# First mixer's attention: the two heads of a pair scored side by side, and the causal mask added into the gate row

## The reference

```
c = jnp.cumsum(logf, axis=-1)
...
    logits = jnp.einsum('bhqd,bhkd->bhqk', qb, k) * scale + cb[..., None] - c[:, :, None, :]
    allowed = (kpos[None, :] <= qpos[:, None]) & (valid[None, :] | (kpos[None, :] == qpos[:, None]))
    p = jax.nn.softmax(jnp.where(allowed[None, None], logits, NEG), axis=-1)
    return jnp.einsum('bhqk,bhkd->bhqd', p, v)
```

## Time and profile before

| | us |
|---|---|
| median of 3 runs | 3825.36 (3823.08 to 3827.70) |
| the profiled execution | 3827.49 |
| its span in the trace | 3825.7 |
| PE busy | 3763.7 |
| DVE busy | 1361.9 |
| POOL busy | 1045.1 |
| ACT busy | 757.2 |

### The profile page before, as it was taken

The page is one execution under the profiler, slowest core; times in us unless marked ns, Lnnn a source line. Parts: engine busy times, 40 slices in busy tenths (PEclk is TensorE's granted clock), DMA queues, the critical chain, the costliest instruction groups (busy, mean ns, idle before and its releaser), DMA issues.

```text
span 3825.7 us, 42159 instructions
## 1 busy us (share of the span) xinstructions
PE 3763.7 (98%) x17657; PEld 2652.7 (69%) x17657; DVE 1361.9 (36%) x2155; ACT 757.2 (20%) x1343; POOL 1045.1 (27%) x919
## 2 busy tenths in 40 slices
PE   8999999999999999999999999999999999999999
PEld 7888677775554588874565444478887557748888
DVE  3221210311121322135634300168823274338861
ACT  2000251222300100012332310010012355230000
POOL 4554100000000155522442100046641020016663
PEclk9999999999999999999999999999999999999999
DMA  4222443223131233222323222223223410023322
GB/s 134 82 86 83 85 67 58 36 34 44 50 66 66 81 85 88 86 84 76 99 83 105 66 77 77 77 77 89 86 91 108 77 45 4 6 56 88 89 83 72
DMA packets 368031, 281.83 MB, mean 74 GB/s; under 512 B 11011, under 2 KB 359811, under 8 KB 367844
## 3 DMA queue, kind: packets, MB, share of 16 engines
q1 hardware_dynamic: 367556, 278.88, 27.5%
q10 hardware_dynamic: 288, 0.27, 0.0%
HBM read 276.44 MB, written 2.69 MB: 73 GB/s over the span
## 4 chain that ended last, share of the span: by engine, by line
PE 97%; DVE 1%; ACT 1%; issue 0%; DMA 0%; POOL 0%; SPq 0%; DVEq 0%; ACTq 0%
PE psum L604 41%; PE psum L1995 14%; PE psum L1309 6%; PE psum L2188 3%; PE psum L1430 3%; PE psum L2886 3%; PE psum L1344 2%; PE psum L1091 1%; PE psum L1121 1%; PE psum L3726 1%; PE psum L1982 1%; PE psum L1087 1%; PE psum L1162 1%; PE psum L3461 1%; PE psum L573 1%; PE psum L2972 1%
## 5 line engine op out<-in xcount | busy, mean ns | idle before, releaser
L604 PE MATMUL psum<-work 128*128 128x256 f32 (+1 forms) x2400 | 551.4, 381 | 0.0
L523 POOL TENSOR_TENSOR work<-weight_ring 128x512 f32<-128x512 f32 x132 | 163.2, 1236 | 1376.5 <-PE psum L604 735.0
L604 PEld LDWEIGHTS psum<-work 128*128 128x128 f32 x2400 | 456.0, 190 | 66.0
L604 PE MATMUL psum<-work,weight_ring 128*128 128x256 f32 (+1 forms) x2080 | 481.8, 381 | 0.0
L604 PE MATMUL psum<-normalized,weight_ring 128*128 128x256 f32 (+1 forms) x2016 | 468.2, 382 | 2.9 <-DVE normalized L724 2.9
L1995 PE MATMUL psum<-normalized,weight_ring 128*128 128x512 f32 x1024 | 451.1, 596 | 0.0
L604 PEld LDWEIGHTS psum<-work,weight_ring 128*128 128x128 f32 x2080 | 395.2, 190 | 57.2
L604 PEld LDWEIGHTS psum<-normalized,weight_ring 128*128 128x128 f32 x2016 | 383.6, 190 | 61.4 <-DVE normalized L724 4.5
L1995 PEld LDWEIGHTS psum<-normalized,weight_ring 128*128 128x128 f32 x1024 | 192.3, 191 | 228.8 <-issue 227.7
L748 DVE TENSOR_TENSOR work<-work,psum 128x512 f32<-128x512 f32 (+1 forms) x100 | 68.7, 687 | 641.7 <-PE psum L604 641.7
L682 ACT ACTIVATE work<-psum 128x256 f32<-128x256 f32 (+1 forms) x100 | 38.5, 385 | 1094.2 <-PE psum L604 1094.2
(11 more groups left out here) (518 smaller groups left out, 4915.9 us busy)
## 6 DMA issues: line engine op xcount, KB each, us to landing
weight_ring<-in_w_in SPq DMA_DIRECT2D x73, 1024.0 KB, 7.7
weight_ring<-in_w_ffn_in SPq DMA_DIRECT2D x88, 512.0 KB, 5.1
weight_ring<-in_ffn_w_up SPq DMA_DIRECT2D x44, 512.0 KB, 4.6
weight_ring<-in_ffn_up SPq DMA_DIRECT2D x44, 512.0 KB, 5.0
weight_ring<-in_w_ffn_out SPq DMA_DIRECT2D x16, 1024.0 KB, 5.2
weight_ring<-in_w_out SPq DMA_DIRECT2D x12, 1024.0 KB, 5.1
work<-decay_sums SPq DMA_DIRECT2D x16, 512.0 KB, 4.1
weight_ring<-in_w_proj_b SPq DMA_DIRECT2D x8, 1024.0 KB, 5.1
```

Source lines behind the costliest of these rows:

```text
L523: own(pool.tensor_tensor(s1, a21, a22, ALU.add))
L604: last = pe.matmul(K.ps[:, self.BANK[m] * T:self.BANK[m] * T + self.H], left(m, p), right(pe, m, p), start=first and p == 0, stop=last_par ...
```

## The change

Of the attention:

- `units()` lists a pair's units by query block from the last to the first, and the two heads of a block next to each other
- the scores of two units (one block, both heads) are issued together at every even turn (`scores_pe`), in pieces of at most 256 columns, head 0 and head 1 in turn, into banks 0 and 1; they wait until DVE has scaled both units before
- the causal mask's product on PE is gone; DVE adds the mask into the gate row's diagonal block ahead of each unit
- the gate rows, the meta scores and a pair's end stand at other turns: the even head's row at turn 7 of the pair before, the odd head's at turn 0 right behind the scores, the meta scores at turn 6 of the pair before, a pair's end one turn earlier each

Of the scan: DVE masks the scb products of both tiles of a pair first and does the rest of both after.

```diff
-        return [(p, h, i) for p in range(FOX_PAIRS) for h in range(2) for i in range(NT)]
+        return [(p, h, i) for p in range(FOX_PAIRS) for i in reversed(range(NT)) for h in range(2)]
...
-                if s > 1:
-                    pe.wait_ge(*S["scaled"](s - 1))
-                pe.matmul(K.bank(s % 2, (i + 1) * P), A(self.q + p * T + i * P, P, half(h)), A(self.k + p * TM, (i + 1) * P, half(h)),
-                          start=True, stop=False, skip_group_check=True)
-                pe.matmul(K.bank(s % 2, P, P, i * P), K.ident[:, :], K.causal[:, :], start=False, stop=True, skip_group_check=True)\
-                    .then_inc(S["scored"].h, 1)
+            more = p + 1 < FOX_PAIRS
+            if s < n and s % 2 == 0:
+                self.scores_pe(pe, s)
+            if s < n and rel == 0:
+                self.forget_bias_pe(pe, 2 * p + 1)
             self.side_until(side, (s + 4) * SIDE)
+            if more and rel == 6:
+                self.meta_scores_pe(pe, p + 1)
+            if more and rel == 7:
+                self.forget_bias_pe(pe, 2 * p + 2)
...
+        if s:
+            pe.wait_ge(*S["scaled"](s))
+        for c in range(0, width, HALF_BANK):
+            w = min(HALF_BANK, width - c)
+            for h in range(2):
+                last = pe.matmul(K.bank(h, w, P, c), A(self.q + p * T + i * P, P, half(h)), A(self.k + p * TM + c, w, half(h)),
+                                 start=True, stop=True)
+                if c + w == width:
+                    last.then_inc(S["scored"].h, 1)
...
+                if s:
+                    dve.wait_ge(*S["scaled"](s))
+                diagonal = A(self.ncb + h * T + i * P, P)
+                own(dve.tensor_tensor(diagonal, diagonal, K.causal[:, :], ALU.add))
+                own.wait()
                 dve.wait_ge(*S["scored"](s + 1))
                 if s > 2:
                     dve.wait_ge(*S["turned"](s - 2))
...
-        for t in N:
+        for both in (N[0:2], N[2:4]):
+            for t in both:
+                b = 4 * (t % 2)
+                dve.wait_ge(*Z["scb"](t + 1))
```

More of the change, by code:

```diff
@@ L876 @@
 PAIR_UNITS = 2 * NT
+HALF_BANK = 256
 SIDE = 7
@@ L1188, in attention_pe, with scores_pe @@
             if s >= PAIR_UNITS:
-                if rel == 2:
+                if rel == 1:
                     self.meta_turn_pe(pe, p - 1)
-                if rel == 4:
+                if rel == 3:
                     self.meta_values_pe(pe, p - 1)
-                if rel == 6:
+                if rel == 5:
                     self.turn_y_pe(pe, p - 1)
-            if rel == 5 and p + 1 < FOX_PAIRS:
-                self.forget_bias_pe(pe, 2 * p + 2)
+    def scores_pe(self, pe, s):
+        K, A, S = self.K, self.A, self.s
+        p, _, i = self.units()[s]
+        width = (i + 1) * P
+        if s:
[7 more added lines that the diff above has]
+                    last.then_inc(S["scored"].h, 1)
     def forget_bias_pe(self, pe, head):
@@ L1201, in forget_bias_pe @@
         p = head // 2
[L1202 to L1206, removed]
+        if head % 2:
+            pe.wait_ge(*S["ncb_copied"](head))
+        else:
             pe.wait_ge(*S["meta_biased"](p + 1))
[L1208 to L1211, removed]
         row = bass.AP(K.ident, head, [[P, FOX_HEADS], [0, P]])
@@ L1216, in meta_scores_pe @@
         K, A, S = self.K, self.A, self.s
[L1217 to L1221, removed]
+        if p == 1:
+            pe.wait_ge(*S["ncb_copied"](2))
+        elif p > 1:
             pe.wait_ge(*S["y_ready"](p - 1))
@@ L1243, in turn_y_pe @@
         pe.wait_ge(*S["tails"](p + 1))
[L1244 removed]
+        pe.wait_ge(*S["ncb_copied"](min(2 * p + 4, FOX_HEADS)))
         pe.wait_ge(*S["meta_copied"](p + 1))
@@ L1496, in attention_act @@
                 Ls = A(self.L + (s % 3) * T, (units[s][2] + 1) * P)
+                if rel == 0:
+                    self.forget_bias_act(act, 2 * p + 1)
                 act.wait_ge(*S["scaled"](s + 1))
@@ L1499, in attention_act @@
                     .then_inc(S["probs"].h, 1)
-                if rel == 1:
-                    self.forget_bias_act(act, 2 * p + 1)
+                if rel == 7 and p + 1 < FOX_PAIRS:
+                    self.forget_bias_act(act, 2 * p + 2)
             if s >= PAIR_UNITS:
-                if rel == 1:
+                if rel == 0:
                     mm = A(self.mm + ((p - 1) % 2) * P, P)
@@ L1506, in attention_act @@
                     act.activation(mm, mm, ACT.Exp, scale=-1.0).then_inc(S["meta_probs"].h, 1)
-                if rel == 2:
+                if rel == 1:
                     act.wait_ge(*S["meta_turned"](p))
                     act.activation(A(self.mt + ((p - 1) % 2) * P, P), K.bank(5, P), ACT.Copy).then_inc(S["meta_copied"].h, 1)
-                if rel == 6:
+                if rel == 5:
                     act.wait_ge(*S["y_turned"](p))
                     act.activation(A(self.q + (p - 1) * T, T), K.bank(5), ACT.Copy).then_inc(S["y_ready"].h, 1)
-            if rel == 5 and p + 1 < FOX_PAIRS:
-                self.forget_bias_act(act, 2 * p + 2)
             for end, name, at in ends:
@@ L1524, in forget_bias_act @@
         if head > 1:
-            act.wait_ge(*S["scaled"](head // 2 * PAIR_UNITS - (4 if head % 2 == 0 else 0)))
+            act.wait_ge(*S["scaled"](head // 2 * PAIR_UNITS - (1 if head % 2 == 0 else 0)))
         act.activation(A(self.ncb + (head % 2) * T, T), self.K.bank(5), ACT.Copy).then_inc(S["ncb_copied"].h, 1)
@@ L1662, in attention_dve @@
         dve.wait_ge(*S["line_stored"](16))
+        self.meta_scores_dve(dve, own, 0)
         for s in range(n + 8):
@@ L1667, in attention_dve @@
                 c, w = self.column(s), (i + 1) * P
-                if rel == 0:
-                    self.meta_scores_dve(dve, own, p)
-                if i == 0:
+                if i == NT - 1:
                     dve.wait_ge(*S["ncb_copied"](2 * p + h + 1))
+                if s:
[3 more added lines that the diff above has]
+                own.wait()
                 dve.wait_ge(*S["scored"](s + 1))
@@ L1677, in attention_dve @@
                                          accum_out=A(self.stat_min + c, 1)).then_inc(S["scaled"].h, 1)
+                if rel == 6 and p + 1 < FOX_PAIRS:
+                    self.meta_scores_dve(dve, own, p + 1)
+                if rel == 7:
+                    self.meta_less_dve(dve, p)
             if s >= PAIR_UNITS:
-                if rel == 0:
-                    self.meta_less_dve(dve, p - 1)
-                if rel == 3:
+                if rel == 2:
                     self.total_dve(dve, own, p - 1)
-                if rel == 5:
+                if rel == 4:
                     self.tail_dve(dve, p - 1)
@@ new lines, in scan_dve @@
+        for both in (N[0:2], N[2:4]):
+            for t in both:
+                b = 4 * (t % 2)
+                dve.wait_ge(*Z["scb"](t + 1))
+                dve.tensor_tensor(A.two(self.si + t * 2 * T, self.rr + t * 2 * T, BLOCKS, 2 * CHUNK, CHUNK),
+                                  K.ps[:, b * T:(b + 2) * T].rearrange("p (x b n) -> p x b n", b=2, n=CHUNK),
+                                  mask(0, 2).rearrange("p x (b n) -> p x b n", n=CHUNK), ALU.mult).then_inc(Z["scb_masked"].h, 1)
+            for t in both:
+                b = 4 * (t % 2)
+                ab = self.bank_pair(b + 2, b + 3)
+                dve.tensor_tensor(self.heads(self.st, t), ab, self.masks_of(4), ALU.mult)
+                dve.wait_ge(*Z["scc"](t + 1))
+                dve.wait_ge(*Z["be_ready"](t + 1))
+                dve.tensor_tensor(self.heads(self.r, t), ab, self.masks_of(5), ALU.mult)
+                dve.tensor_tensor(self.heads(self.k, t), ab, self.masks_of(6), ALU.mult).then_inc(Z["ab_masked"].h, 1)
+                products = K.ps[:, b * T:(b + 2) * T].rearrange("p (x b n) -> p b x n", b=2, n=CHUNK)
+                dve.tensor_tensor(by(A(self.ar + t * T, T), CHUNK), products[:, 0], mask(2), ALU.mult)
+                dve.tensor_tensor(A.blocks(self.rr + t * 2 * T + CHUNK, BLOCKS, 2 * CHUNK, CHUNK), products[:, 1], mask(3), ALU.mult)\
+                   .then_inc(Z["scc_masked"].h, 1)
```

9 lines of the change are left out of this document (2 added, 7 removed).

## The result

The changed kernel took **3781.39 us** (median of 4 runs, 3778.22 to 3782.29) against 3824.96 for before on the same chip. The ratio is 0.9884 with a 95% interval of 0.9867 to 0.9901, 43.6 us less. The forecast was 3780, from a gain of 45.3.

What follows compares the result with a forecast made beforehand. PE was taken to bound the kernel, with slack on DVE. Attention's 41.3 us (13.8 + 11.4 + 17.1, less losses) plus the scan's 4.0 made 45.3, from 3825.4 to 3780 us; range 3773 to 3794.

Steps and rivals of the forecast that it cites:

- rival A: Whole kernel: the forecast itself, all three parts of the change pay, 3774 to 3786 us; chance 0.70.
- The mask, 13.8 us: Attention on PE: dropping the mask's product removes 64 units of 0.215 us, 13.8 us saved.
- The row halves, 17.1 less 0.7: Attention scores on PE: two heads side by side cost one head's columns, 17.1 us saved, less 0.7 for lost overlap.
- Changes of height, 11.4: Attention on PE: changes of weight height fall from 145 to 88, at 0.20 us each, 11.4 us saved.
- 1.0 (0.7 + 0.2 + 0.1): Attention losses: 0.7 us of lost overlap, 0.2 net behind turn 56, 0.1 for the start.
- The split at turn 56: Attention's end, without side work: PE saves 5.4 us, waits add 2.8, a shorter drain returns 2.6; net loss 0.2.
- The hand-over: Scores' stricter wait for DVE: hidden by 3.0 us of side work; rival D, waits at all 32 groups, 3793 us, 0.09.
- The scan, 4.0: Scan: masking both tiles first ends the last masks 3.3 us earlier; up to 1.6 more from the clock; 4.0 taken.
- a sign that the prediction had ruled out: Scan: second scc should start about 0.5 us behind the first, and no record be stretched to 0.42.
- Strict order (B): Attention scores: matmuls start only in program order, costing 6.0 us in all, 3786 us; chance 0.10.
- no overlap (C): Attention scores: neighbouring pieces block each other, so only 13.8 + 11.4 + 4.0 = 29.2 us are saved, 3796; chance 0.06.

Runs made afterwards that it cites:

- experiment 4: Changed kernel with the causal mask's product back on PE and no mask addition on DVE: 3800.66 us, attention stage 314.6 (311.2 without the low clock).
- experiment 2: Changed kernel with head 1's scores reading head 0's partitions, so both use the same row half: 3801.03 us, attention stage 315.5 (312.1 at full clock).
- experiment 5: Changed kernel with DVE adding the mask four or eight times over instead of once: 3793.19 and 3801.57 us.
- experiment 1: Each edit alone against the kernel before (3827.73 us): changed attention with old scan order 3783.80; old attention with new scan order 3823.56.
- heads-apart run: Changed kernel with all of head 0's score pieces issued first, then all of head 1's, instead of in turn: 3779.47 us, attention stage 295.3.
- four additions: Changed kernel with DVE adding the mask four times over, about 1.0 us more on DVE ahead of each unit: 3793.19 us.

## Why the prediction was right

The time was 3781.4 for 3780 and rival A held. By its own steps:

- **What bounds it.** Right. The chain of work stayed on PE, and DVE's additions did not reach the end.
- **The mask, 13.8 us.** Right: 15.9 came back with the mask, of which 1.6 are changes of height that the term does not hold and 0.5 are open (experiment 4).
- **The row halves, 17.1 less 0.7.** The 17.1 is right, 16.9 by experiment 2. The 0.7 for lost overlap was not needed: a group of 512 columns takes 1.07 from start to start, which is 0.853 plus one load (0.107) and one change (0.10), as in the earlier trace rows. The 1.26 that the prediction names counts the change ahead of the group too.
- **Changes of height, 11.4.** Not tested alone. 41.0 measured in the stage less 16.9 and 13.8 leaves 10.3 for them and all losses. With the full 11.4 the losses are 1.1, where the prediction had 1.0 (0.7 + 0.2 + 0.1). Since the 0.7 was not lost in the overlap, where those 1.1 lie is open, and that they match is in part luck.
- **The split at turn 56** was wrong in its parts. Turn 56 to the end took 19.9 us, 6.1 less than before instead of 5.2, and the turns ahead of it 34.9 less instead of 36. The new order of the blocks has, by turn 56, five transposes and five value products more behind it than the old, 5 x 0.11 + 5 x 0.22 = 1.65 us of work that moved ahead of the cut. With it the prediction would have had 6.9 and 34.4; the 0.8 and 0.5 that are left, of opposite sign, have no run of their own. The sum doesn't see the cut. PE's recorded waits behind turn 56, ahead of the last transposes, are 1.6 us and were 1.3 before.
- **The hand-over** is covered, with at least 1 us a unit in hand up to turn 56 (experiment 5).
- **The scan, 4.0.** 3.3 in the trace up to the doubling, which is the 3.3 that the prediction gives the masks of the last tile. What it had above that, 0.7 of a possible 1.6, was for the clock in the doubling's first tile, and nothing came of it: the clock fell there again, from 3210.7 for 3.4 us (from 3258.1 for 3.4 before), behind a stall of 1.89 us where it had been 3.74. Ahead of that it fell at the end of a stall of 1.93, for 3.4 us instead of 6.8, and records were stretched to 0.42 (line below), a sign that the prediction had ruled out. So the shorter stalls do not keep the clock up, and part of the 3.3 is the shorter stretch (experiment 1).

```profile
3197.18 0.45 PE L3510 MATMUL psum<-identity,work 128*128 128x128 f32 x1 [1.93 <-DVE work L3883]
...
3197.42 0.42 PE L3511 MATMUL psum<-identity,work 128*128 128x128 f32 x1
```

- **Strict order (B), no overlap (C)** are both refuted by runs. The Trainium skill (TensorE: Matmul & The Clock Gate, Part 3: Packing small matmuls) has matmuls start and end strictly in program order. The heads-apart run differs: head 1's first record starts ahead of three that stand before it, 0.013 us after head 0's first.
- What the prediction did not have is the clock at the attention's start, up to 3.4 us in a run that it catches. The fastest of the four runs (3778.22) is the one that was profiled, and it had the full clock there; the other three are 2.5 to 4.1 us longer, and such a fall would account for up to 3.4. They were not profiled, so this is argued and not shown. That the forecast came within 1.4 us is in part luck, since the four runs alone lie 4 us apart.

## What to carry to other kernels

Where a product uses half of the rows, issue it next to one that uses the other half: in this kernel two cost what one costs (1.07 us against 1.92), whatever the pieces' size or order within a few records. Count the changes of weight height as well, 0.2 us each by the earlier trace rows, and group or place products so that fewer are needed; a product that is cheap by its columns (0.213 us for 128) can cost more by the two changes around it (0.4). And before adding a stricter wait, measure what the waiting engine has queued in front of it: with four additions the 3 us of side work still hid it, while two score products in the turns without side work waited 1.9 us.

## What the runs showed that I had not expected

The order of four records did not matter (head 1 starts 0.013 us after head 0 instead of 0.007), so this kernel need not interleave by hand. The granted clock fell to half, for 6.8 us in five of six cases and 3.4 in one, where PE had waited no more than 0.5 us and streamed products of 16 and 64 rows behind that wait. In the scan it fell at or behind stalls of 1.9 us as it had with 3.7.
